# Six modulation chunks of a two-model kernel move from the attention stage to stand behind two sums of squares

## The reference, cut to what matters

```
# end of the first model
x = x + mod_x[:, 5, None] * expert_choice_ffn(hx, w_router, w_exp_gate, w_exp_up, w_exp_down)
x = rms_norm(x, g_final)

# second model
cond = jax.nn.silu(c)
for layer in range(2):
    mod = (cond @ ada_w[layer] + ada_b[layer])[:, None, :]        # 1024 -> 6144
    sh1, sc1, g1, sh2, sc2, g2 = jnp.split(mod, 6, axis=-1)
    hh = rms_norm_2(x, norm1_g[layer]) * (1.0 + sc1) + sh1
    mix = nsa_mixer(hh, ...) if layer == 0 else rglru_mixer(hh, ...)
    x = x + g1 * mix
    hh = rms_norm_2(x, norm2_g[layer]) * (1.0 + sc2) + sh2
    x = x + g2 * swiglu(hh, ffn_w_in[layer], ffn_w_out[layer])
```

## Time and profile before

| | us |
|---|---|
| median of 3 runs | 1793.6 (1793.29 to 1796.42) |
| span of the profiled execution, first to last instruction | 1790.9 |
| PE busy | 1489.2 (83%) |
| DVE busy | 787.4 (44%) |
| ACT busy | 578.9 (32%) |
| POOL busy | 33.8 (2%) |

### The profile page before, as it was taken

How to read it: one execution, slowest core, us unless ns; L and a number is a source line. 1 busy time by engine, 2 the same in 40 slices (tenths; PEclk the granted TensorE clock), 3 DMA queues, 4 the chain that set the end, 5 groups by cost and what they waited for, 6 DMA issues and landing times. The chain is left out here.

```text
span 1790.9 us, 26831 instructions
## 1 busy us (share of the span) xinstructions
PE 1489.2 (83%) x11250; PEld 1165.0 (65%) x11250; DVE 787.4 (44%) x1166; ACT 578.9 (32%) x834; POOL 33.8 (2%) x39
## 2 busy tenths in 40 slices
PE   6999997889966565565755799988999989889999
PEld 3788975578942121121211698448999989779999
DVE  4352445476641000000000756565655475865553
ACT  4332134575221101010100531464333354743332
POOL 2000020000000000000000000000000000100000
PEclk8999998999968787887687897899999999899999
DMA  9554456642729999999999552862545534335540
GB/s 397 236 228 174 163 212 237 229 145 98 279 99 419 429 427 427 426 429 427 427 429 425 213 189 94 321 244 94 184 177 183 187 141 166 141 126 182 187 165 24
DMA packets 46749, 437.94 MB, mean 245 GB/s; under 512 B 5200, under 2 KB 5456, under 8 KB 6064
## 3 DMA queue, kind: packets, MB, share of 16 engines
q1 hardware_dynamic: 45792, 430.99, 61.0%
q0 software_dynamic: 560, 5.01, 0.7%
q10 hardware_dynamic: 288, 0.32, 0.1%
HBM read 435.25 MB, written 1.05 MB: 244 GB/s over the span
## 5 line engine op out<-in xcount | busy, mean ns | idle before, releaser
L677 PE MATMUL bank<-H_r,ring_r 128*128 128x256 f32 x3488 | 511.9, 288 | 18.5 <-DVE H_r L1611 18.5
L677 PEld LDWEIGHTS bank<-H_r,ring_r 128*128 128x128 f32 x3488 | 466.6, 196 | 24.3 <-issue 22.6
L677 PE MATMUL bank<-arena_r,ring_r 128*128 128x256 f32 x2776 | 407.0, 291 | 38.1 <-DVE ring_r L1634 26.8
L1634 DVE TENSOR_TENSOR ring_r<-ring,ring_r 128x2048 fp32r<-128x2048 f32 x136 | 319.1, 2348 | 223.3 <-ACT ring_r L1324 223.0
L677 PEld LDWEIGHTS bank<-arena_r,ring_r 128*128 128x128 f32 x2776 | 377.2, 197 | 54.4 <-issue 26.6
L1324 ACT ACTIVATE ring_r<-ring 128x2048 fp32r<-128x2048 f32 x136 | 259.5, 1909 | 221.1 <-PE bank L677 176.8
L1013 PE MATMUL bank<-ring,arena 128*32 128x512 f32 x1024 | 171.6, 807 | 126.2 <-DMA ring<-in_w 124.3
L1013 PEld LDWEIGHTS bank<-ring,arena 128*32 128x32 f32 x1024 | 34.5, 129 | 251.7 <-DMA ring<-in_w 146.7
L1895 DVE TENSOR_TENSOR arena<-arena,bank 64x512 f32<-64x512 f32 x16 | 11.1, 691 | 280.8 <-ACT arena L1426 280.8
L1426 ACT ACTIVATE arena<-bank 64x512 f32<-64x512 f32 x16 | 9.4, 589 | 368.8 <-PE bank L1013 368.8
L1040 PE MATMUL bank<-ring,arena 128*32 128x256 f32 x1024 | 85.8, 495 | 26.6 <-DMA ring<-in_w 21.4
(11 more groups left out here) (245 smaller groups left out, 1253.4 us busy)
## 6 DMA issues: line engine op xcount, KB each, us to landing
ring<-in_w SPq DMA_DIRECT2D x216, 1024.0 KB, 4.9
ring<-in_w SPq DMA_DIRECT2D x96, 2048.0 KB, 25.6
ring<-in_bias POOLq DMA_DIRECT2D x1, 2048.0 KB, 10.5
consts<-in_consts POOLq DMA_DIRECT2D x1, 1439.0 KB, 9.8
X<-in_x SPq DMA_DIRECT2D x1, 1024.0 KB, 5.5
arena<-in_ctx SPq DMA_DIRECT2D x1, 1024.0 KB, 7.9
arena<-in_decay POOLq DMA_DIRECT2D x1, 1024.0 KB, 11.6
out_t<-X SPq DMA_DIRECT2D x4, 256.0 KB, 2.0
```

What stands on the lines that cost most here:

```text
L677: i = nc.tensor.matmul(o, lhsT, rhs, start=start, stop=stop, skip_group_check=grouped)
L1634: v.tensor_tensor(r(lo), lo, r(hi), ALU.subtract).then_inc(lo_ready, 1)
```

## The change

`blocks(LAST_BLOCKS, MOD_BLOCKS)` is put into the filler list already behind the experts, and three of its steps are taken behind `sum_sq 2` and three behind `sum_sq 3`: `mod 6 0` to `mod 6 5`. The NSA loop takes two steps per iteration as before, from the 24 that are left, so that the filler ends with iteration 11 and not with iteration 14. `mod_row 6` stands in iteration 1 (before: 4), `mod_row 7` in iteration 6 (before: 9), `mod_row 8` in iteration 11 (before: 14).

```diff
--- before.py
+++ after.py
@@ -127,13 +127,16 @@
     s += [("gather", k) for k in range(KT)]
     s += [("experts",)]
     s += [("combine", p) for p in range(4)]
-    s += [("sum_sq", 2), ("apply", 2), ("sum_sq", 3), ("apply", 3)]
+    fill += blocks(LAST_BLOCKS, MOD_BLOCKS)
+    for n in (2, 3):
+        s.append(("sum_sq", n))
+        take(3)
+        s.append(("apply", n))
 
     s += [("nkv", 0), ("nkv", 1), ("nqk", 0), ("nqk", 1), ("cmp", 0, 0), ("cmp", 0, 1), ("cmp", 1, 0),
           ("cmp", 1, 1), ("cmp_k",), ("cmp_v",), ("nnorm", 0), ("nnorm", 1)]
     s += [("nqk", 2), ("nqk", 3), ("nnorm", 2), ("nqk", 4), ("nnorm", 3), ("nqk", 5), ("nnorm", 4), ("nsa_parts",),
           ("nv", 0), ("nnorm", 5), ("nv", 1), ("nnorm", 6), ("ngate",), ("cmp_s",)]
-    fill += blocks(LAST_BLOCKS, MOD_BLOCKS)
     for i in range(PAIRS + LAG + 1):
         take(2)
         if i < PAIRS:
```

## The result

| | before | changed |
|---|---|---|
| median of 7 runs each, us | 1793.29 (1786.47 to 1797.99) | 1803.08 (1801.76 to 1806.8) |
| span of the profiled execution, us | 1790.9 | 1800.3 |

The ratio is 1.0057, with a 95% interval of 1.0041 to 1.0072: the change costs 9.8 us. The forecast was +10.0.

What follows compares the result with a forecast made beforehand. PE, busy 83%, was taken to bound the kernel outside its breaks. +15.6 us up to the projections, 0 there and -5.6 in the NSA stage gave +10.0, 1803.6 us, range 1797.6 to 1809.0.

Steps and rivals of the forecast that it cites:

- The total: Whole kernel: +10.0 us, a time of 1803.6 us, with chance 0.72.
- the head: Stretch from the last expert product's start to `nkv 0`; the terms up to the projections summed to +15.6 us.
- the projections: Stretch from `nkv 0` to the NSA stage's first filler: no cost.
- the NSA stage: From its first filler to `nsa_out 0`: -5.6 us, bounds -9 to -2.5.
- The wait of the splits: Ahead of `sum_sq 2`, ACT's two weight copies wait for later loads, so the squares start 16.8 us later.
- Rival 1: ACT's splits ahead of `sum_sq 2` wait for nothing; only gains remain, -8.7 us, 1784.9 us; chance 0.06.
- `sum_sq 2` at the lower clock: After a longer PE break `sum_sq 2` runs mostly at the lower clock, 5.6 us: +1.9, bounds 0 and +2.6.
- The filled breaks: Three chunks behind each sum fit free; `sum_sq 3` runs at full clock, -3.0 us, and `nkv 0` gains about 0.1.
- The stops for ACT's copies: In the NSA stage, PE's stops for ACT's block copies with the lower clock behind them: -1.1 us in the middle.
- the units without filler: NSA iterations 12 to 14 lose their cover while ACT copies transposes: +1.3 us.
- rival 3: Removed NSA chunks were cover: stage only -2.5, total +13.1, or +16.1 (1809.7 us) with `sum_sq 3` slow; chance 0.10.
- Rival 2: NSA stage gives back 9 us as stops and low clock go, loads 2 us early: +4.8, 1798.4 us; chance 0.12.

Runs made afterwards that it cites:

- e1: Kernel before, with only ACT's two splits ahead of `sum_sq 2` also waiting for the loads in places 6 and 7; 1809.86 us, ratio 1.0091.
- e4: Changed kernel with only three chunks moved, all behind `sum_sq 2` and none behind `sum_sq 3`; 1785.55 us, ratio 0.9955.
- e3: Changed kernel with the same steps, but the weights of `nkv 0` and `nkv 1` loaded ahead of the six chunks; 1795.82 us, ratio 1.0003.
- e7: e4 with the weights of `nkv 0` and `nkv 1` loaded first, ahead of the three chunks; 1779.56 us, ratio 0.9913.
- e6: Changed kernel with iteration 0 of the NSA loop taking one filler step and not two; 1800.11 us, ratio 1.0036.
- e5: Kernel before with iteration 0 of the NSA loop taking one filler step and not two; no chunk leaves the stage; 1782.7 us, ratio 0.9943.
- e8: e7 with five chunks, three behind `sum_sq 2` and two behind `sum_sq 3`; 1785.37 us, ratio 0.9944.
- e2: Kernel before with `mod 6 0` to `mod 6 5` left out, products and loads; other 24 filler steps two per NSA iteration; 1790.52 us, ratio 0.9983.

## Why the prediction was right, point by point

**The total** came within 0.2 us (+9.8 for +10.0), and so close a hit is luck. In the profiles the head fell 0.9 us short of the forecast, the projections cost 0.9 more, the NSA stage gave back 0.9 less, and 1.6 us ahead of the first cut and behind the last went the other way, which no term had. What was right is the sign and its cause.

**The wait of the splits**, the term that carries the sign, is shown by taking it alone (e1, +17.0 us), by its dose (from the last expert product to the squares, against before: e4, three places further, +7.5; e1 and the changed kernel, six places, +14.7 and +15.25; 2.5 us per place), and by removing it with the filler left in place (e3 and e7: head 23.6 and 23.5). Rival 1, in which the splits wait for nothing, is out. The size was a little off: the squares started 19.64 us after the last expert product for 4.39 before, +15.25 and not +16.8, since the loads landed 1.5 us earlier against the last expert product; the forecast had carried their times over from before. In the trace of before the eight loads land 2.5 us apart but for one step of 4.4, beside a load that GpSimd issued at 991.35; in that of the changed kernel the largest step is 2.9. That GpSimd's load makes the step is not shown.

**`sum_sq 2` at the lower clock**: 6.04 us for the 5.6 forecast; e1 had 5.78, e6 6.07 and e4, behind a break of 7.19 us, 6.46. The forecast's lower rate, 0.39 us for one instruction, was too fast: it came from the 6.24 us of `sum_sq 3`, and the granted clock in that product was 0.59 on average, so part of it ran at the full clock. Twice the 0.23 us of the full clock is 0.46, and twelve such and four at 0.23 make 6.4, an estimate. The Trainium skill, "TensorE: Matmul & The Clock Gate", section "What's actually happening", has it that the watch on the array's activity runs freely, from which the forecast made a range of 3.69 to 6.24 us. Lengths that vary from 5.78 to 6.46 in four kernels agree with a free phase, but no run behind such a break came near the low end, and e4 lies above the high one.

**The filled breaks**: `sum_sq 3` ended 8.1 us after `sum_sq 2` as forecast (8.0), in place of 10.9. By e1 the filler is owed 1.7 us of this and not 3.0, and without filler `sum_sq 3` took 5.19 us (e5) to 6.24, so its share is 1.5 to 2.5 us. With filler it took 3.72 us in five kernels and 5.32 in e8, so a filled break keeps the clock often and not always. The argument for it was weaker than it looked: I took one break of 1.96 us, followed by a product of 3.72 us, as proof that such a break keeps the clock. In nine of ten profiles the product behind that break of 1.9 us took 5.1 us or more; in two of the nine (e2 and e8) the granted clock was at 0.50 in the break already, in the other seven it was at 1.00 there and fell behind it. Only the execution of before had 3.72.

**The projections**: 0 forecast, +0.9 seen. It is the clock and not the edit's loads. The last 48 projection instructions took 1.1 us more, at a mean granted clock of 0.59 for 0.68 (7.90 us at 1097.71 in the profile of before, 8.99 at 1111.17 in that of the changed kernel), and the rest of the stretch took 0.2 less. In e5, which has the order of before up to the NSA stage, they took 8.69 us, and 7.87 in e1, which has the same order but for the wait.

**The NSA stage**: -4.7 us for -5.6. PE was busy 6.4 us less in the stage and stood 1.7 us more. The stops for ACT's copies came to 7.9 us for 7.3 before (6.8 forecast; the first was 3.81, not 2.7), the stop for DVE at the splits was 1.67 for 1.30, and the units without filler cost 0.6 more in waits for ACT's copies of the transposes, not 1.3, so that little of rival 3 is there. e2 has the same shortening with nothing behind the sums (-3.9), so it belongs to the filler's places. The sum was near for this change, but I had priced the stops by the parity of the unit ahead of `mod_row`. e4 and e5 show that its place within the pair decides, and that it was worth 12 us, more than the change itself. Rival 2 named an effect that exists: stops and low clock can go, by moving the filler an odd number of steps. The change moved it six, and they stayed.

## What to carry to other kernels

When the order of use is also the order of loading, moving a step renumbers all loads behind it: look for whoever waits in order for a load by its place, here two copies on ACT that stand ahead of the moved work in the list. Filler belongs in breaks only if nothing ahead of the break waits for what it pushes back. And where a buffer must be handed over by another engine, put other work between the last user and the next: shifting the list by one step was worth more (11.8 us) than filling two breaks.

## What the runs showed of the hardware

The granted clock makes single executions differ at the same place with the same code. `sum_sq 3` behind an unfilled break took 6.24, 5.41, 6.16 and 5.19 us in four kernels, at mean granted clocks of 0.59, 0.68, 0.60 and 0.71; behind a break of 2.25 us with filler it took 3.72 us in e3 and e7 (1.00) but 5.32 in e8 (0.69). The kernel before spread over 14 us in 29 runs; e4, without the long stops, over 3.4 us in 12. That the stops make the spread is not shown: e1 kept them and spread over 3.9 us in six runs, and e7 had none and spread over 6.8 in six.
